# A transformer block pair on one Trainium2 core: k ahead of q, modulation chunks spread over three stages, a new order in the layer norm, root steps through PSUM

## What is computed

```python
# block 1
x = x + 0.5 * swiglu(rms_norm(x, ffn1_norm), w_gate, w_up, w_down)
h = rms_norm(x, mix_norm)
q, k, v, qi, ki, wi, u = split(h @ w_in)
q = rope(rms_norm(q, q_norm), pos)          # per head of 64
k = rope(rms_norm(k, k_norm), pos)
attn = dsa_attention(q, k, v, qi, ki, wi, top_k)     # the 128 best keys by an index score
pooled = einsum(multiscale_pool(u), pool_w) * pool_scale
x = x + concat(attn, pooled) @ w_out
...
# block 2
mod, mod_c = silu(c) @ w_mod + b_mod, silu(c_ctx) @ w_mod[:, :2048] + b_mod[:2048]
h_c = ctx * (1 + scale_c) + shift_c          # ctxkv: keys and values of the context
x = layer_norm(ALPHA * x + gate1 * mixer(...), ln1_g, ln1_b)
h = x * (1 + scale2) + shift2
x = layer_norm(ALPHA * x + gate2 * conv_ffn(h), ln2_g, ln2_b)
```

## Time and profile before

| what | us |
|---|---|
| median of 3 runs | 1839.51 |
| lowest and highest | 1839.11, 1843.90 |
| the profiled execution | 1840.77 |
| its span, first to last instruction | 1839.0 |
| PE busy, share of the span | 1778.3, 97% |
| DVE, ACT, POOL busy | 996.5, 674.5, 807.0 |
| granted TensorE clock, mean share | 0.981 |

### The profile page before, as it was taken

How to read it: one execution, slowest core, us unless ns; L and a number is a source line. 1 busy time by engine, 2 the same in 40 slices (tenths; PEclk the granted TensorE clock), 3 DMA queues, 4 the chain that set the end, 5 groups by cost and what they waited for, 6 DMA issues and landing times.

```text
span 1839.0 us, 26347 instructions
## 1 busy us (share of the span) xinstructions
PE 1778.3 (97%) x8981; PEld 1504.2 (82%) x8981; DVE 996.5 (54%) x1628; ACT 674.5 (37%) x1389; POOL 807.0 (44%) x642
## 2 busy tenths in 40 slices
PE   7999999999989999999999999899999899999996
PEld 6888778888767888888888888699988788888886
DVE  4214874767896467242124358466567764551545
ACT  4322222243457433223233223555532452332332
POOL 3544444557853355544445555200034265545550
PEclk9999999999999999999999999999999899999998
DMA  6434462634211345433323333100012134333321
GB/s 201 124 102 150 149 183 69 188 92 122 70 46 47 106 135 184 148 92 101 111 83 102 112 92 95 54 1 2 1 55 83 47 89 140 92 92 104 91 80 46
DMA packets 279698, 178.45 MB, mean 97 GB/s; under 512 B 6264, under 2 KB 258356, under 8 KB 279476
## 3 DMA queue, kind: packets, MB, share of 16 engines
q1 hardware_dynamic: 265348, 149.35, 28.0%
q10 hardware_dynamic: 14256, 27.87, 4.5%
HBM read 175.11 MB, written 2.10 MB: 96 GB/s over the span
## 4 chain that ended last, share of the span: by engine, by line
PE 69%; issue 18%; DVE 8%; POOL 3%; ACT 2%; DVEq 0%; POOLq 0%; ACTq 0%
PE ps L688 68%; POOL wL L620 3%; DVE mod_acc L1670 2%; DVE tA L525 1%; PE ps L1096 0%; ACT rel L1391 0%; DVE acc L1637 0%; DVE actL L1723 0%; ACT actH L1353 0%; DVE x L1720 0%; DVE out_nat L2247 0%; ACT wH L1289 0%; DVE mod_acc L1668 0%; DVE out_nat L2261 0%; DVE hidL L1696 0%
## 5 line engine op out<-in xcount | busy, mean ns | idle before, releaser
L620 POOL TENSOR_TENSOR wL<-raw,wH 128x512 fp32r<-128x512 f32 (+2 forms) x560 | 747.4, 1358 | 973.4 <-ACT wH L1289 972.3
L688 PE MATMUL ps<-actH,wH 128*128 128x512 f32 (+1 forms) x1312 | 514.8, 392 | 10.7 <-DVE actL L2128 7.9
L688 PE MATMUL ps<-actL,wH 128*128 128x512 f32 (+1 forms) x1312 | 508.5, 388 | 0.0
L688 PE MATMUL ps<-actH,wL 128*128 128x512 f32 (+1 forms) x1312 | 508.2, 387 | 0.0
L1289 ACT ACTIVATE wH<-raw 128x512 fp32r<-128x512 f32 (+2 forms) x560 | 312.6, 608 | 343.8 <-PE ps L688 332.7
L688 PEld LDWEIGHTS ps<-actH,wH 128*128 128x128 f32 x1312 | 250.8, 191 | 61.9 <-DVE actL L2128 5.6
L688 PEld LDWEIGHTS ps<-actH,wL 128*128 128x128 f32 x1312 | 250.6, 191 | 49.9
L688 PEld LDWEIGHTS ps<-actL,wH 128*128 128x128 f32 x1312 | 250.8, 191 | 49.1 <-issue 0.7
L688 PE MATMUL ps<-hidH,wH 128*128 128x512 f32 (+1 forms) x720 | 268.3, 373 | 0.0
L688 PE MATMUL ps<-hidL,wH 128*128 128x512 f32 (+1 forms) x720 | 267.1, 371 | 0.0
L688 PE MATMUL ps<-hidH,wL 128*128 128x512 f32 (+1 forms) x720 | 267.1, 371 | 0.0
(11 more groups left out here) (307 smaller groups left out, 2056.1 us busy)
## 6 DMA issues: line engine op xcount, KB each, us to landing
mod_raw<-in_w_mod ACTq DMA_DIRECT2D x24, 1024.0 KB, 6.0
raw<-in_w_in SPq DMA_DIRECT2D x48, 512.0 KB, 3.7
raw<-in_ffn_w_gate SPq DMA_DIRECT2D x44, 512.0 KB, 3.8
raw<-in_ffn_w_up SPq DMA_DIRECT2D x44, 512.0 KB, 3.8
raw<-in_w_up SPq DMA_DIRECT2D x44, 512.0 KB, 3.8
raw<-in_ffn_w_down SPq DMA_DIRECT2D x32, 512.0 KB, 4.0
raw<-in_w_out SPq DMA_DIRECT2D x16, 512.0 KB, 4.0
raw<-in_w_down SPq DMA_DIRECT2D x16, 512.0 KB, 4.0
```

What stands on the lines that cost most here:

```text
L620: nc.gpsimd.tensor_tensor(wL[:, b:b + w // 2], raw[:, b:b + w // 2], wH[:, b:b + w // 2].bitcast(F32), ALU.subtract).then_inc(lo_ready, 1)
L688: return nc.tensor.matmul(out, a, b, start=first, stop=last)
```

## The change

1. **Chunks.** Chunks 0 and 1 of the modulation go to f1_down0, ahead of the drains of its tiles 0, 2, 5 and 6. Chunks 2 and 3 stay in f1_up1, half a chunk per turn. PE's sums stand behind tile 4 of f1_down0, tiles 0 and 8 of f1_up1, and tile 1 of f1_down1. The transfers move with them, the loops concerned are written out.
2. **Row root of the mixer.** `row_sums(1)` comes behind slab 1 of ctxkv. idx waits for the root alone (rn). PE's spreading goes into bank 7 behind slab 0 of pool, and DVE's copy to rB behind the rotation of the index tiles; `pooling` and the index scores still wait for that copy.
3. **k ahead of q.** The stages q and k change places, and with them drains, squares and roots. DVE takes k's root first, then picks eight more rounds than it did before q's work, rotates q tiles 0 and 1 unscaled and scales them later (the scale is one number per head and commutes with the rotation). POOL rotates k tile 0 ahead of the v slabs and k tile 1 between them, scales both, waits until DVE is done with q tiles 0 and 1, and then does tiles 2 and 3 of both k and q.
4. **Start of attention 1.** The two pool products come ahead of the logits; ACT drains v's banks 1 and 3 first, then copies the turned q and k, then the other two; an Exp of one zero stands ahead of v's drains; ACT's copies of the pool products and the last split of out1 move behind the first Exp of the attention.
5. **Roots through PSUM.** In `rsqrt` the running value stands in PSUM for the rows of the mixer and of f2, the heads of q and k, and the layer norm. No step then reads two tensors from SBUF. The step count stays eleven; the layer norm's moments get one instruction more.
6. **The layer norm.** Low parts of tiles 4 to 7 of the first half and of all of the second go from DVE to POOL. On DVE the sums of the second half move back behind the first tiles; on PE `moments(1)` comes in behind tile 4 of the first pass over three slabs, and `spread_moments(1)` behind tile 1 of the pass over slab 3.

The core of the diff:

```diff
...
+    rows("k", w_in, ATT, ATT, 2)
     rows("q", w_in, 0, ATT, 2)
-    rows("k", w_in, ATT, ATT, 2)
     rows("v", w_in, 2 * ATT, ATT, 2)
     columns("out1", t["w_out"][0], 0, KT)
...
+    CTX_SUMS = {("f1_down0", 1, 0): 0, ("f1_up1", 0, 0): 1, ("f1_up1", 2, 0): 2, ("f1_down1", 0, 1): 3}
     ACT_BEFORE = {"f1": 0, "f2": 2 * KT, "f3": 5 * KT}
...
+    DVE_LOWS = 4
...
+        def key_turned(q):
+            pool.wait_ge(qk_sq, q + 1)
+            rotated(G, link, k1, 1, q, sq)
+        def key_scaled(q):
+            pool.wait_ge(k_scaled, 1)
+            times_scale(G, k1, k_scale, q).then_inc(k_rot, 1)
...
+        def normal_low(n):
+            half, k = n // KT, n % KT
+            pool.wait_ge(shifted, n + 1)
+            pool.wait_ge(act_hi, 4 * KT + n + 1)
+            G.tensor_tensor(half_of(actL, k, half), aff[:, (n % 2) * HS:][:, 0:HS], half_of(actH, k, half).bitcast(F32),
+                            ALU.subtract).then_inc(act_low, 1)
         for st in stages:
-            if st["name"] == "q":
+            if st["name"] == "k":
                 lows(st, 0, then=pooling)
-            elif st["name"] == "out1":
-                pool.wait_ge(k_scaled, 1)
-                heads_rotated(G, chain, k1, 1, sq, k_scale[:], k_rot)
-                loop(pool, 0, st["its"], lambda i, st=st: lows(st, i))
+            elif st["name"] == "v":
+                key_turned(0)
+                lows(st, 0, slots=(0, 1, 2))
+                key_scaled(0)
+                key_turned(1)
+                lows(st, 0, slots=(3,))
+                key_scaled(1)
+                pool.wait_ge(qk_rot, 2)
+                for q in (2, 3):
+                    key_turned(q)
+                    key_scaled(q)
+                    rotated(G, link, q1, 0, q, sq)
+                    times_scale(G, q1, q_scale, q).then_inc(q_rot, 1)
             else:
                 if st["name"] == "merge":
...
-                loop(pool, 0, st["its"], lambda i, st=st: lows(st, i))
+                begun = 0
+                if st["name"] == "f3_up0":
+                    lows(st, 0)
+                    for n in range(DVE_LOWS, 2 * KT):
+                        normal_low(n)
...
+                            moments(1)
+                        if (half, js, k) == (0, (3,), 1):
+                            spread_moments(1)
+        def ctx_sums(name):
+            def after(i, j):
+                if (name, i, j) in CTX_SUMS:
+                    mod_sums(CTX_SUMS[name, i, j], True)
+            return after
...
+                    feature_tiles(f"f1_down{n}", hidH, hidL, (hid_ready, hid0 + f0), K=nf,
+                                  after=ctx_sums(f"f1_down{n}"), peel=2, paired=True)
                     continue
                 feature_tiles(f"{name}_down{n}", hidH, hidL, (hid_ready, hid0 + f0), K=nf,
...
             mm.then_inc(slab_done, 1)
-            if j == 0:
+            if j == 1:
                 row_sums(1)
-            if j == 2:
-                spread_rows(1)
         def before_idx():
             pe.wait_ge(act_ready, 2 * KT)
-            pe.wait_ge(stat_out, 2)
...
+            if j == 0:
+                pe.wait_ge(drained_a, drain_base["idx"] + 4)
...
-        token_tiles("q", ATT, 4, lambda: pe.wait_ge(idx_rel, 12))
-        token_tiles("k", ATT, 0, lambda: pe.wait_ge(drained_a, drain_base["pool"] + 4))
-        token_tiles("v", ATT, 4, lambda: pe.wait_ge(drained_a, drain_base["q"] + 4))
+        token_tiles("k", ATT, 4, lambda: pe.wait_ge(idx_rel, 12))
+        token_tiles("q", ATT, 0, lambda: pe.wait_ge(drained_a, drain_base["pool"] + 4))
+        def before_v():
+            pe.wait_ge(drained_a, drain_base["k"] + 4)
+            pe.wait_ge(k_scaled, 1)
+        token_tiles("v", ATT, 4, before_v)
...
+            for src, b in ((q1, 1), (k1, 3)):
+                if src is k1:
+                    pe.wait_ge(k_rot, q + 1)
+                elif q < 2:
+                    pe.wait_ge(qk_rot, q + 1)
+                else:
+                    pe.wait_ge(q_rot, q - 1)
                 for pair in range(4):
...
+        pool_products()
+        attention(group1, 0, prob1, probT1, lambda: pe.wait_ge(drained_a, drain_base["v"] + 4), during1)
...
-            if early:
-                early()
-            for q in range(ST):
+            for n, q in enumerate(order):
+                if n == 2 and early:
+                    early()
                 nc.scalar.activation(into[:, q * width:(q + 1) * width], bank(bank0 + q, width), ACT.Copy,
                                      scale=rn[:, q:q + 1]).then_inc(drained_a, 1)
...
-        token_stage("v", 4, v1, ATT, early=lambda: tile_columns(0))
+        nc.scalar.activation(exp_of_zero[:], zero[:], ACT.Exp).then_inc(exp_begun, 1)
+        token_stage("v", 4, v1, ATT, early=lambda: tile_columns(0), order=(1, 3, 0, 2))
+        def after_first_exp():
+            pool_high(0)
+            pool_high(1)
+            split(stage_of["out1"], 0, SLOTS - 1)
...
+            if 2 <= n < DVE_LOWS + 2:
                 act.wait_ge(act_ready, 5 * KT + n - 1)
+            elif n >= 2:
+                act.wait_ge(act_low, n - 1 - DVE_LOWS)
...
+            a, y = small[:, 64:64 + w], out if room is None else room
+            link(V.tensor_scalar(y.bitcast(I32), v.bitcast(I32), 1, None, ALU.logical_shift_right))
+            link(V.tensor_scalar(y.bitcast(I32), y.bitcast(I32), -1.0, RSQRT_MAGIC, ALU.mult, ALU.add))
             for step in range(3):
-                link(V.tensor_tensor(a, out, out, ALU.mult))
-                link(V.scalar_tensor_tensor(a, a, -0.5, v, ALU.mult, ALU.mult))
-                ins = V.scalar_tensor_tensor(out, a, 1.5, out, ALU.add, ALU.mult)
+                link(V.tensor_tensor(a, v, y, ALU.mult))
+                link(V.scalar_tensor_tensor(a, a, -0.5, y, ALU.mult, ALU.mult))
+                ins = V.scalar_tensor_tensor(out if step == 2 else y, a, 1.5, y, ALU.add, ALU.mult)
...
+            rsqrt(rn[:], small[:, 0:ST], ST, last=(rn_ready, n + 1), room=bank(4, ST, 64) if n else None)
+        def rows_spread(n, b=5):
...
-            dve.wait_ge(row_bcast, n + 1)
-            V.tensor_copy(rB[:], bank(5)).then_inc(stat_out, 1)
-            dve.wait_ge(stat_out, n + 1)
+            row_root(n)
+            rows_spread(n)
         def add_term(term, count):
...
+            def body(i, hook=None):
                 for j in range(SLOTS):
                     m = i * 4 + j
+                    if hook:
...
                     V.scalar_tensor_tensor(tile(x, m), bank(j), 0.5, tile(x, m), ALU.mult, ALU.add).then_inc(drained_v, 1)
-            chain.loop(0, 2, 0, body)
+            if name == "f1_down0":
+                for i in range(2):
+                    body(i, first_chunks)
+            else:
+                chain.loop(0, 2, 0, body)
             dve.wait_ge(drained_v, d0 + KT)
+        def first_chunks(i, j):
+            if (i, j) == (0, 0):
+                dve.wait_ge(silu_c_ready, 2)
+            if (i, j) == (1, 1):
+                mod_columns(0, True)
+            if (i, j) in ((0, 0), (1, 1)):
+                mod_products(i, 0, True)
+            if (i, j) in ((0, 2), (1, 2)):
+                mod_products(i, 1, True)
...
-        pick(2, 0, 10)
...
-            rsqrt(out, small[:, 0:32], 32, last=last)
-        head_scales(0, small[:, 128:160])
-        heads_rotated(V, chain, q1, 0, tA, small[:, 128:160], qk_rot)
-        pick(2, 10, 13)
-        head_scales(1, k_scale[:], last=(k_scaled, 1))
-        pick(2, 13)
-        pick(3, 0, 5)
+            rsqrt(out, small[:, 0:32], 32, last=last, room=bank((0, 4)[n], 32))
+        dve.wait_ge(drained_a, drain_base["k"] + 4)
+        head_scales(1, 0, k_scale[:], (k_scaled, 1))
+        pick(2, 11)
+        pick(3, 0, 2)
+        for q in range(2):
+            dve.wait_ge(qk_sq, ST + q + 1)
+            rotated(V, link, q1, 0, q, tA)
+        dve.wait_ge(drained_a, drain_base["q"] + 4)
+        head_scales(0, ST, q_scale, (q_scaled, 1))
+        for q in range(2):
+            times_scale(V, q1, q_scale, q).then_inc(qk_rot, 1)
+        pick(3, 2, 5)
         def pool_low(g):
...
+            again = bank(5, 2, 16)
+            link(V.tensor_tensor(md[:, two], ps[:, 5, 2 * half:2 * half + 2], c[:, two], ALU.subtract))
+            link(V.tensor_tensor(again, ps[:, 5, 2 * half:2 * half + 2], c[:, two], ALU.subtract))
+            link(V.tensor_tensor(md[:, two], md[:, two], again, ALU.mult))
             link(V.scalar_tensor_tensor(small[:, two], ps[:, 5, 4 + 2 * half:6 + 2 * half], LN_EPS, md[:, two],
                                         ALU.add, ALU.subtract))
-            rsqrt(rn[:, two], small[:, two], 2, last=(rn_ready, 4 + half))
+            rsqrt(rn[:, two], small[:, two], 2, last=(rn_ready, 4 + half), room=bank(5, 2, 20))
         def normal(n):
...
```

217 lines of the change are left out of this document (118 added, 99 removed).

## The result

The changed kernel takes 1813.58 us (median of 4 runs, 1812.67 to 1815.21) against 1839.49 for the kernel before: a ratio of 0.9847, 95% interval 0.9835 to 0.9859. The forecast was 1813.9, with a range of 1806 to 1827.

What follows compares the result with a forecast made beforehand. PE was taken as the bound (busy 1778.3 of 1839.0 us), so only its waits and half-clock stretches could be gained. 10.3 + 6.0 - 3.0 + 5.3 + 7.0 = 25.6 off 1839.51 gave 1813.9 us, range 1806 to 1827.

Steps and rivals of the forecast that it cites:

- Part 1: Modulation chunks moved to f1_down0: PE's four waits (5.4) and three clock stretches (5.1) go; 10.3 us gained, ends 7 to 10.5.
- Part 3: Start of k's stage: POOL, delayed behind copy to rB, makes PE wait for wL; loses 3.0 us (0 to 6).
- part 4: k ahead of q and start of attention 1: shorter PE waits and pool products; 5.3 us gained, ends 3 to 6.5.
- Part 6: Layer norm: shorter PE waits (3.5, plus 0.5 smaller) and one clock stretch gone (3.0); 7.0 us gained, ends 4 to 9.8.
- Part 2: Mixer's row root: row_sums one slab later removes PE waits before idx and index turns; 6.0 us gained, ends 3.5 to 7.
- part 5: Roots through PSUM: a root can shorten by 1 to 2 us where POOL is busy, already counted elsewhere.
- Something smaller is late next: Start of attention 1: after the removed waits another wait, around logits and ACT's copies, limits; 6.2 us upper end becomes 5.3.
- rival 3: POOL's pause before qk_rot delays its tiles, so PE waits in attention; slower, 1846 us, chance 0.03.
- The rule on two SBUF inputs: Layer norm: DVE steps with two SBUF inputs contend with POOL's lows; gain would be 3 us instead of 7.
- signs of being wrong: Listed trace signs against the forecast; in the layer norm, `centre` or `add_square` above 1 us while POOL subtracts.
- Rival 2: Waits go but clock still falls; modulation, row root and layer norm keep only waits: gain 15.4, 1824 us, chance 0.13.
- Rival 1: POOL later than reckoned: slower chain or late q tiles, PE waits 6 us, clock falls twice; 1821 us, chance 0.14.

## Why the prediction was right, point by point

The total is nearer than its parts. Parts 1 and 3 came out 0.9 and 1.3 better than their sizes, parts 4 and 6 0.2 and 0.8 worse, and two pieces that should not have moved lost 0.5. That 26.3 us of span stand against 25.6 is luck to that extent. Parts 1, 2 and 6 were tested by undoing them or pieces of them; k ahead of q and the order at the start of attention 1 were not undone, so part 4 rests on the two profiles alone, but for the Exp and ACT's first copies.

**Part 1** was sized 10.3 and measured 11.23, confirmed by its undoing. The steps held: 5.4 of waits and three stretches, 10.5 together; the 0.7 that are left I can't place. The cover at tile 4 was put at 1 us and was 0.4. The products there ran at 1.36 us each (10.87 for eight) against 1.12 in the earlier trace rows, and every one has two SBUF inputs. That place is the weakest of the change: one tile earlier costs 9.6.

**Part 2** came out at 5.96 for 6.0, but two of its inner sizes were wrong. I gave the order nearly all and PSUM 0.2. With the roots in SBUF the gain shrinks to 1.0: with row_sums one slab later 5.7 us are left between the sums' end (400.82) and idx (406.52), and a root of 2.1 us fits into that, one of 8.6 does not. (The same root took 4.8 us in the kernel before, from 411.85 to 416.63, since GpSimd had pauses between its lows there. PSUM without the new order was not run.) The step that failed is the sentence in part 5 that a root loses 1 to 2 us; it loses 6.5 in eleven steps. The rows shown had the 1.03 of a single step, and I did not multiply it by the eleven steps that can stand beside GpSimd's work.

**Part 3** was sized 3.0 and measured 1.68: the wait was 1.48 instead of 2.2 to 2.4, and no clock stretch followed. GpSimd started 3.5 us later against the index turns (3.6 forecast), but its window sums took 41.7 us (432.80 to 474.52) instead of 42.4 (446.20 to 488.60), and that is the difference. The wait stands at q's first matmul, the second of the two stages, and not at k's, where the prediction put it. The mechanism, GpSimd's unbroken chain from the copy to rB, is shown by the sum that was moved behind q's first lows; the forecast's own case, 2.53 with a stretch, appeared when the chunks were put back.

**Part 4** gave 5.08 for 5.3. "Something smaller is late next" was 2.28 us for the first turned prob, behind ACT's copies of the pool products and its split. That is 1.7 more than the 0.60 of before, where I had taken off 0.9 in all; what made up for it is a second low stretch, 3.4 us at 551.4 before, which I had not counted and which is gone. Moving these copies behind the first heads did not remove it: it split into 1.40 and 0.38. The table's load cost nothing, as forecast, because the Exp of a zero puts it at 510.78, in time that ACT has; left where it was, it would have cost 1.1 in the new order.

**GpSimd's pause** (rival 3) had the cover I gave it. On POOL, the pause for DVE's tiles 0 and 1, the last step of q tile 2, and the first lows of out1 behind the two pairs; then PE's turn of tile 2:

```profile
514.96 1.55 POOL L530 TENSOR_TENSOR sq<-k,ropeT 128x256 f32<-128x256 f32 x2 [8.67 <-DVE q L559]
...
524.64 1.04 POOL L559 TENSOR_TENSOR q<-q,small 128x512 f32<-128x512 f32 x1
...
536.26 9.88 POOL L630 TENSOR_TENSOR wL<-raw,wH 128x512 fp32r<-128x512 f32 x8
...
544.21 0.61 PE L1108 MATMUL ps<-const,q 128*128 128x128 f32 x4
```

The pairs took 21.3 us (21.8 forecast), and PE needed tile 2 23.4 us after the v stage, 18.5 after GpSimd was done with it.

**Part 6** was sized 7.0 and measured 6.24. The first wait fell by 1.9 (forecast 1.3 to 2), the 2.69 to 0.89 (forecast 1). But the waits behind the first grew, and all waits together fell by 2.6 where I had put 4.0. The clock made up for most of that, which is luck: it was at 0.50 for 3.41 us where I kept 10, a gain, and for 3.41 more behind the 2.04 us wait at 1452.17, where before none had followed the same wait: the 1.61 of the table. The rule on two SBUF inputs, which would have made it 3, did show in the first half, as one of my signs of being wrong (`add_square` above 1 us) in these rows of DVE:

```profile
1415.99 1.18 DVE L2212 TENSOR_TENSOR sq<-sq,sq 128x256 f32<-128x256 f32 x1
...
1419.64 1.38 DVE L2254 TENSOR_TENSOR actL<-aff,actH 128x256 fp32r<-128x256 f32 x1
```

But it was the weight slabs' lows that met them, which were there before. GpSimd's new low parts begin at 1426.53 and stand beside normals, which read PSUM and one SBUF tensor and took 0.41 to 0.42 throughout. So the rule agrees with these rows and did not bear on what moved.

Rival 2 (the waits go, the clock falls anyway) is out for f1 and half true for the layer norm. Rival 1's cause, a slower chain of GpSimd, did not show in the changed kernel (41.7 us against 42.4); with the chunks back it was 0.5 us slower, and that with its later start cost 2.7.

## What to carry to other kernels

Before a chain of tiny vector steps is left on the path, look at what GpSimd does beside it and count the steps that read two SBUF tensors: moving one operand to PSUM took this root from 8.6 to 2.1 us in the new order, and only with it did the order pay. Price a wait of PE with the clock behind it, and as a range: here a wait of 1.85 us cost 3.6 with its stretch, one of 5.13 cost 9.6, one of 10.01 cost 12.9, and one of 2.04 cost nothing more in some executions. When a step moves ahead of others, ask which engine it sets free to run, and whose operands that engine then meets.

## What the runs showed of the hardware that I had not expected

The length of a low stretch of the clock tends to grow with the wait of PE before it, but it is not a function of it. All stretches lay at 0.50, that is 1.2 GHz. Behind 1.85 and 3.18 us came 3.4. With the waits of 5.13 and 10.01 us came 10.2 and 13.7, but these began inside the waits: 9.05 and 5.9 us of them fell on PE's work and cost 4.5 and 2.9, so the longer wait had the cheaper stretch. The waits for the modulation sums of 0.79 to 0.98 us were followed by 3.4 in two cases (0.82 and 0.92) and by nothing in two, and the 1.73 at the index turns before by nothing. The small matmuls of the sums did not lower the clock by themselves: without a wait ahead of them (137.29) it stayed at 1.00. The same 2.28 us wait in the same order of work was followed by 6.8 in the changed kernel's two executions and by 3.4 in most variants, the 4.33 us wait ahead of the second attention likewise by 6.8 or 3.4, and the 2.04 us wait in f3_up0 by 3.4 or by nothing. What decides between them stays open; it makes 0.6 to 1.6 us of difference at a place, and a difference of that size that goes with a stretch's length is not put down to a change here.

The other surprise is how far apart causes can lie. With the chunks back in f1, a wait at q's start, 250 us later, was 2.53 instead of 1.48, and with the roots in SBUF it was 0.49. The instructions there are the same. In the second case PE had simply been held up ahead of it, so that GpSimd was ahead; in the first GpSimd got rB 0.6 us later and its sums took 0.5 us longer, which I put down to how DVE's two-input steps and GpSimd's meet, without a run that shows it.
